# Row transfers of a DMA-paced decoder step on one Trainium2 core: the last norm's weights and four result tiles moved 8 partitions at a time

## The reference, cut to what matters

```python
def rms_norm(x, g):
    xf = x.astype(jnp.float32)
    y = xf * lax.rsqrt(jnp.mean(xf * xf, axis=-1, keepdims=True) + EPS)
    return (y * g.astype(jnp.float32)).astype(x.dtype)
...
        idx = jnp.take_along_axis(cidx, sel, axis=-1)
        gate = jax.nn.softmax(top, axis=-1)
        h = jnp.einsum('td,thkd->thk', xt, u_tab[idx]).astype(jnp.float32)
        a = (jax.nn.gelu(h, approximate=False) * gate).astype(xt.dtype)
        return jnp.einsum('thk,thkd->td', a, v_tab[idx])
...
    y_prompt = rms_norm(xp, g_final)
    y_sample = rms_norm(xs, g_final)
```

## Time and profile before

| | |
|---|---|
| median of 3 runs | 1707.67 us (1706.31 to 1708.52) |
| profiled execution, its own time | 1707.81 us |
| its span, first to last instruction | 1706.0 us |
| PE busy | 1301.5 us (76%) |
| DVE busy | 1165.7 us (68%) |
| ACT busy | 810.4 us (48%) |
| GpSimd busy | 641.3 us (38%) |
| moved by DMA | 657.35 MB, mean 385 GB/s |
| of this by the gathers' queue (q0) | 604.28 MB, 85.7% of 16 engines' span |
| by SP's queue (q1) | 51.68 MB, 8.1% |

### The profile page before, as it was taken

How to read it: one execution, slowest core, us unless ns; L and a number is a source line. 1 busy time by engine, 2 the same in 40 slices (tenths; PEclk the granted TensorE clock), 3 DMA queues, 4 the chain that set the end, 5 groups by cost and what they waited for, 6 DMA issues and landing times.

```text
span 1706.0 us, 21619 instructions
## 1 busy us (share of the span) xinstructions
PE 1301.5 (76%) x7069; PEld 475.1 (28%) x7069; DVE 1165.7 (68%) x2795; ACT 810.4 (48%) x2337; POOL 641.3 (38%) x584
## 2 busy tenths in 40 slices
PE   9999878987889776677777776776767677667665
PEld 4455523433444222122322111111111111111110
DVE  2544578887667677787777777777667677677764
ACT  1434366775444354455555454445444445444443
POOL 0000044434434344444444443444444444444441
PEclk9999998899999988899988777878888877888866
DMA  9433699999999999999999999999999999999995
GB/s 353 168 138 134 232 400 422 408 374 422 421 421 421 420 398 420 421 403 421 419 421 412 422 421 421 421 422 421 421 421 421 421 405 422 421 421 420 422 419 220
DMA packets 99041, 657.35 MB, mean 385 GB/s; under 512 B 12576, under 2 KB 17568, under 8 KB 22368
## 3 DMA queue, kind: packets, MB, share of 16 engines
q0 software_dynamic: 83056, 604.28, 85.7%
q1 hardware_dynamic: 15872, 51.68, 8.1%
HBM read 652.71 MB, written 4.19 MB: 385 GB/s over the span
## 4 chain that ended last, share of the span: by engine, by line
DMA 44%; PE 26%; ACT 11%; DVE 10%; issue 7%; POOL 2%; ACTq 0%; DVEq 0%; SPq 0%; POOLq 0%
DMA R<-in_peer_uv,R 43%; PE ps L2009 10%; PE ps L1543 6%; DVE R L1462 4%; PE ps L1802 3%; ACT L911 2%; ACT R L920 2%; PE ps L1515 2%; ACT R L915 1%; POOL R L641 1%; ACT R L911 1%; ACT L826 1%; DVE R L1285 1%; DVE R L1286 1%; DVE R L1288 1%
## 5 line engine op out<-in xcount | busy, mean ns | idle before, releaser
L2009 PE MATMUL ps<-R 64*64 64x512 f32 x4536 | 732.3, 725 | 370.4 <-ACT R L920 364.9
L641 POOL DMA_INDIRECT R<-in_peer_uv,R x567 | 627.8, 1107 | 966.4 <-PE ps L2009 762.8
L1462 DVE CUSTOM_DVE_ANT_0 R<-R 128x1024 f32<-128x1024 f32 x567 | 689.3, 1225 | 382.4 <-DMA R<-in_peer_uv,R 368.3
L911 ACT ACTIVATE R<-R 128x1 f32<-128x1 f32 x576 | 115.9, 201 | 594.6 <-DVE R L1462 585.2
L2009 PEld LDWEIGHTS ps<-R 64*64 64x64 f32 x4536 | 134.5, 149 | 713.3 <-ACT R L920 627.1
L920 ACT ACTIVATE R<-R 128x64 f32<-128x64 f32 x576 | 200.4, 348 | 54.3 <-ACT R L915 1.5
L1802 PE MATMUL ps<-A,R 128*128 128x256 f32 (+1 forms) x640 | 224.8, 479 | 0.7 <-ACT R L802 0.7
L915 ACT ACTIVATE R<-R 128x1 f32<-128x1 f32 x576 | 169.8, 295 | 21.2 <-ACT R L911 0.4
L1802 PEld LDWEIGHTS ps<-A,R 128*128 128x128 f32 (+1 forms) x640 | 96.3, 201 | 261.9 <-issue 260.4
L1543 PE MATMUL ps<-A,R 128*128 128x512 f32 (+1 forms) x256 | 101.1, 547 | 0.0
L911 ACT ACT_TABLE_LOAD x60 | 77.0, 1283 | 9.0 <-DVE R L1462 8.0
(11 more groups left out here) (288 smaller groups left out, 936.6 us busy)
## 6 DMA issues: line engine op xcount, KB each, us to landing
R<-in_peer_uv,R POOLq DMA_INDIRECT x567
A<-in_w_pq SPq DMA_DIRECT2D x8, 1024.0 KB, 10.3
A<-in_w_in SPq DMA_DIRECT2D x3, 2048.0 KB, 20.5
R<-in_w_out SPq DMA_DIRECT2D x5, 1024.0 KB
x_res<-in_x_prompt SPq DMA_DIRECT2D x6, 512.0 KB, 12.9
R<-in_w_out SPq DMA_DIRECT2D x1, 3072.0 KB
R<-in_x_promptT SPq DMA_DIRECT2D x4, 512.0 KB, 9.2
R<-in_w_cq SPq DMA_DIRECT2D x2, 1024.0 KB, 10.9
```

The costliest lines, as they stand in the source:

```text
L641: pool.indirect_dma_start(slots[slot_of[g]], None, I["peer_uv"][:, :], bass.IndirectOffsetOnAxis(ap=idx[:, b % 4, k:k + 1], axis=0)).then_ ...
L911: act.activation(hgelu[:, b % 2, col], hdot[:, b % 2, col], ACT.Gelu).then_inc(gelu_ready, 1)
L1462: dve.tensor_tensor_reduce(u, u, xn(t), 1.0, 0.0, ALU.mult, ALU.add, hdot[:, b % 2, k:k + 1]).then_inc(u_used, 1)
L2009: ins = pe.matmul(bank(2 * (t % 2) + q)[rows], diag[tokens, g % DIAGS, :], v_rows[slot_of[g]][tokens, c * 512:(c + 1) * 512], start=first, ...
```

## The change

g_fin is loaded by 16 transfers of 8 partitions each instead of one of 128. Tile 0 (64 rows) is stored by 8 transfers of 8 rows, tiles 1 to 3 by 16 each, instead of one each. g_fin's loads have a semaphore of their own, `ld_fin`, for which `final` waits in place of `ld_ffn`. The bytes, the places and the order are the same, and tile 4 is stored as before.

```diff
+        ld_fin = sem("ld_fin")
...
             sp.wait_ge(l_sc, TILES)
-            load(g_fin, I["g_final"].rearrange("(a d) -> a d", a=1).broadcast_to([P, D]), ld_ffn)
+            for r in range(0, P, 8):
+                sp.dma_start(g_fin[r:r + 8], I["g_final"].rearrange("(a d) -> a d", a=1).broadcast_to([8, D]))\
+                  .then_inc(ld_fin, 16)
             for t in range(TILES - 1):
                 sp.wait_ge(fin_y, t + 1)
                 if t == 0:
                     dst, src = O["y_s"].rearrange("a b d -> (a b) d"), xr(0)[0:NS]
                 else:
                     dst, src = O["y_p"][0, (t - 1) * P:t * P], xr(t)
-                sp.dma_start(dst, src).then_inc(stored, 16)
+                for r in range(0, width(t), 8):
+                    sp.dma_start(dst[r:r + 8], src[r:r + 8]).then_inc(stored, 16)
...
-            sp.wait_ge(stored, 16 * (4 + TILES + 1))
+            sp.wait_ge(stored, 16 * (4 + NS // 8 + 3 * (P // 8) + 2))
...
-                dve.wait_ge(ld_ffn, 48)
+                dve.wait_ge(ld_fin, 16 * (P // 8))
```

## The result

The changed kernel takes 1716.43 us (median of 6 runs, 1714.18 to 1719.0); the kernel before took 1707.59 us beside it (median of 6, 1706.02 to 1708.52). The ratio is 1.0052, 95% interval 1.0041 to 1.0063, so it is slower by 7 to 11 us. The profiled execution took 1716.03 us, with a span of 1714.2 us where before had 1706.0.

What follows compares the result with a forecast made beforehand. The DMA engine that finishes last, under a full queue of gathers, was taken to bound the kernel; 6.4 + 2.6 = +9.0 us on the profiled 1707.81 us gave 1716.8, stated as 1716 us, range 1710.5 to 1727.

Steps and rivals of the forecast that it cites:

- The DMA engines bound the kernel, the last of them sets the end: From about 900 us on, gathers keep DMA queues full; each us more on the last engine lengthens the kernel a us.
- Eight engines a transfer, always the same, the last one among them: In g_fin's load and the split stores, the same eight engines carry all 72 transfers; last engine among them, chance 0.78.
- completion packets: Over all split transfers, each of the eight engines posts 72 instead of 5, at 8.5 ns each: +0.57 us.
- Tile 0, +0.65 us, and tiles 1 to 3, +3.85 us: At the stores, row packets on half as many engines: +0.65 us for tile 0, 1.28 us three times for the others.
- G_fin, +1.31 us, its completions 0.13 us, and +2.6 us of contention: At g_fin's load: half the engines, +1.31 us; writes into 8 neighbouring partitions double its 16 packets, +2.6 us.
- The sum, +9.0 us: On the last engine: 6.4 us of packets and completions plus 2.6 us of slowed g_fin writes.
- Nothing for the stores' reads: At the stores of tiles 0 to 3, reading few partitions adds nothing: packets stay at 0.16 us.
- Rival 1: At the stores, few partitions slow reads too: 1726 us with doubled packets, 1746 by the skill's ports; chance 0.10.
- SP's 67 issues hidden: On SP, 67 more issues of 0.35 us cost nothing; g_fin lands over 100 us before DVE needs it.
- Rival 2: The last engine is not one of the eight: end moves 0 to +3 us, 1708 to 1711 us; chance 0.09.
- rival 3: Last engine outside the eight, whose own straggler is more than 6 us ahead: faster, 1702 to 1704 us; chance 0.03.
- The tail: After the last gather issue: a longer stretch, with a DMA share near 0.5 in it instead of 0.06.

## Why the prediction was right, point by point

- **The DMA engines bound the kernel, the last of them sets the end**: shown. Taking the stores away gave their packets' time back (4.1 us of 4.5), and the compute engines' work stayed the same. One reading of the rows was careless: the share is at 9 tenths from slice 6 on, not 14, and the last slice reads 5.
- **Eight engines a transfer, always the same, the last one among them**: shown by the completion packets and by the steps that grow with the rows per engine.
- **Tile 0, +0.65 us, and tiles 1 to 3, +3.85 us, with completion packets 0.06 and 0.38 us**: the sum had 0.71 for tile 0 and 1.41 for each other. Measured: 0.64, then 1.20 and 1.28 in after; 0.59, 1.27 and 1.22 with the stores alone. The data term (1.28) fits alone; the completion packets show in none of these steps, so that term was too much. Tile 3's own step has the kernel's end in it, 0.90 and 0.20 us. All four stores: predicted 4.9, measured 4.0 in after and 3.3 with the stores alone.
- **G_fin, +1.31 us, its completions 0.13 us, and +2.6 us of contention**: together 4.0. The steps read 3.2 us in after and 3.3 with g_fin alone, and read up to 2 us low. The lost work says more: 1.31 us for half the engines and 4.4 or 3.5 of contention are 5.7 or 4.8 (an estimate, which takes it that the last engine is hindered as the mean of them is), and g_fin alone made the median 5.3 us longer. So the term was some 1 us too small by these numbers, and its mechanism as told was not right. I took it that g_fin's own packets double on the eight engines. The DMA view after, 863 to 880 us, to be read against the earlier trace rows:

```profile
q0 software_dynamic: 653, 4.76, 90.6%
q1 hardware_dynamic: 256, 0.52, 11.0%
```

Q1: 0.110 x 17 x 16 = 29.9 us; less 128 completions at 8.5 ns, 28.8 us over 128 packets, 0.225 us each instead of 0.16. Q0: 0.906 x 17 x 16 = 246.4 us for 4.76 MB, 581 rows of 8 KB, 0.424 us each; before, in the 6 us of the earlier trace rows, 0.793 x 6 x 16 = 76.1 us for 240 rows (1.97 MB), 0.317:

```profile
q0 software_dynamic: 272, 1.97, 79.3%
```

So g_fin's packets grew by 0.065 us, 16 of them 1.0 us an engine, where I had 2.6; the gathers' packets, over the whole of the 17 us and all 16 engines, by a third. In engine time that is 62 us on the gathers and 8 on the load, together 70 / 16 = 4.4 us: the contention fell mostly on the gathers. My range for it started from the right row: x_sample's load goes into 64 partitions, and g_fin in two transfers of 64 fell to 274 GB/s too.
- **The sum, +9.0 us**: the medians differ by 8.84 us. That it is so near is in part luck: the stores were put 0.9 us too high and g_fin about 1 us too low, and the two errors cancel.
- **Nothing for the stores' reads**: right. In the stretch of tile 1's store after, 1048 to 1056 us, the DMA view says:

```profile
q0 software_dynamic: 414, 3.02, 89.9%
q1 hardware_dynamic: 177, 0.36, 11.7%
```

0.117 x 8 x 16 = 15.0 us for 88 packets of 4 KB and 89 completions: 0.16 us each after 0.8 us for the completions, and 423 GB/s in that window. With the stores by 4, from 1041 to 1053 us, q1's 91 packets take 4.1%: 0.041 x 12 x 16 = 7.9 us, for 46 rows and 45 completions, 0.16 us a row again. Rival 1 is refuted, at 8 and at 4 partitions.
- **SP's 67 issues hidden**: right, 5.38 us for 16, and g_fin was in long before it was needed.
- **Rival 2 and rival 3** fall with the last engine's place: had it been outside the eight, the stores by 4 would have cost some 5 us and not 13.
- **The tail**: I expected a longer one, since seven engines would be late beside the last. It has the same length and shape. Ten us of it, before and after:

```profile
1683.00:1693.00 10.00, 5.38 (x36) 0.93 (x32) 4.93 (x8) 3.52 (x13) 0.00 (x0) 0.84 0.14 59
```

```profile
1691.00:1701.00 10.00, 8.05 (x36) 1.22 (x32) 4.93 (x8) 3.47 (x14) 0.00 (x0) 0.50 0.14 59
```

A gather is issued when an older one has landed, and it lands with the last engine. The last gather's issue moved by 7.4 us with all the rest (1675.98 us before, 1683.33 after), so the others had their work later too. What they were spared shows earlier, as idle time some tens of us behind a store, where before has none. The 10 us from 1070 us, before and after (from 1200 us the after has 0.96 too, at 372 GB/s):

```profile
1070.00:1080.00 10.00, 7.85 (x54) 2.36 (x50) 5.05 (x10) 4.69 (x17) 6.84 (x7) 1.00 1.01 420
```

```profile
1070.00:1080.00 10.00, 8.85 (x48) 2.22 (x40) 8.34 (x16) 7.08 (x20) 5.36 (x4) 0.86 0.96 378
```

What stays open is why small writes hinder the gathers. Shown is that they do, that reading one row many times is not the cause (8 different rows did it too), and that spreading 8 partitions changes nothing. That the order of the partitions matters at 16 rests on one execution of each, and it fits the blocks and the ports alike; neither is shown.

## What to carry to other kernels

- Where DMA engines bound a stretch, cost a transfer on the engine that is last, not on their mean: rows that it carries times the packet's time. Splitting a transfer of 128 partitions into ones of 8 or 4 piles it on few engines, and one of those may be the last.
- In this kernel split writes into SBUF beside a full queue of gathers cost the gathers more than the writes themselves; split reads cost nothing but their place on few engines.
- Ask for each transfer whether it must run in the full stretch. Four stores held back until the last gather had landed cost nothing there; the kernel became 0.4% faster (0.2 to 0.5%), 4 us of it the stores' packets.

## What the runs showed of the hardware that was not expected

- Writes of 524 KB in 16 transfers of 8 partitions brought the whole core's DMA rate from 420 to between 296 and 334 GB/s for some 17 us at a share of 1.02; the gathers' 8 KB packets went from 0.317 to 0.424 us. In 30 us from the issue the 16 engines lost 3.5 to 5.1 us of work to it. Transfers of 16 neighbours (3.4 us) and of 64 neighbours (2.4) did it too, and least every eighth partition by 16 (1.8).
- Reads from 8 and from 4 partitions at a time kept 0.16 us a packet.
- Eight neighbouring partitions took SP 0.34 us to issue, as did 128 (0.33), but 16 neighbours took 0.45 (8 issues in 3.57 us) and 64 took 0.49 to 0.58; with strided partitions 16 issues took 9.79 us, 0.61 us each (the timeline of SP in the strided kernel):

```profile
860.31 9.79 SPq L593 DMA_DIRECT2D R<-in_g_final  x16
```
